# A three-block model on one core: turned values by transposing transfers instead of TensorE

## The chip, the cores and the metric

The kernel runs on one core of one Trainium2 chip. The metric is the device time of one execution in microseconds (us). The core's engines are TensorE (PE in the rows; PEld is its weight load), VectorE (DVE), ScalarE (ACT), GpSimd (POOL) and SyncE (SP), each with its own queue of instructions, and 16 DMA engines that all queues share.

## The reference

The kernel computes two networks in a row on a sequence of 256 tokens with 2048 channels, in fp32. The first has two layers (differential attention and an S5 state-space mixer), each followed by an MLP; the second is one hybrid layer (forgetting attention and an RWKV-7 scan). What bears on the change is:

```python
def sqrelu_mlp(h, w1, w2):
    a = jax.nn.relu(h @ w1)          # 2048 -> 8192
    return (a * a) @ w2              # 8192 -> 2048

for i in range(DEPTH):               # 2 layers; i = 0 attention, i = 1 S5 with a GLU
    h = rmsnorm(x, norm_mix[i])
    x = x + mix
    x = x + sqrelu_mlp(rmsnorm(x, norm_mlp[i]), mlp_w1[i], mlp_w2[i])
return rmsnorm(x, norm_final)        # then the second network, which begins with a norm
```

## The kernel before

**Weights.** Every product with a weight matrix runs in chunks of 512 output columns. A chunk is eight units of 256 rows of the weight, 512 KB each. SP loads a unit into one of four buffers `raw`; ScalarE casts it to its upper part `wH` (four buffers); VectorE subtracts to get the lower part `wL` (`split`). PE multiplies the activation's upper and lower parts (`xH`, `xL` or `hH`, `hL`) with them: 12 matmuls of 128x512 a unit, eight with `wH`, then four with `wL`, for two blocks of 128 tokens (`product`, L1025 to L1042). SP loads the next unit when its `raw` buffer has been split, ScalarE casts when PE has used the unit four before (`unit_used`). Chunks alternate between two pairs of PSUM banks `acc[0]` and `acc[1]`.

**Turning.** A product needs its activation with the channel on the partitions; norms and squares leave it with the token there. PE turns it with transposes into PSUM (`turn`, L1044 to L1049): a turn here is 512 channels of 256 tokens, eight transposes. ScalarE then copies the upper part out of PSUM (`high`), VectorE subtracts the lower part (`low`), which frees the PSUM bank (`group_free`).

**Norms.** A norm's operand is made a quarter (512 channels) at a time, while the product before it still runs: VectorE adds a chunk to `X`, multiplies by the gain into `xn` (`lead_gain`), PE turns the quarter in the middle of the next chunk (`lead_mid`), ScalarE and VectorE take it out (`lead_high`, `lead_low`). The factor 1/rms comes in later. The fourth quarter is turned after the second unit of the next product's first chunk; the first unit of that chunk waits until the first three quarters are there (`lead_first`).

**MLPs.** Each has four blocks of eight chunks: four with `w1`, whose results ScalarE passes through a relu and VectorE squares into `stg`, then four with `w2`. In the first MLP all four squares of a block are turned by PE, one in the middle of each next chunk. Between its chunks VectorE, ScalarE, PE and GpSimd also make the tables of the S5 mixer. In the second MLP PE turns only the fourth. For the other three GpSimd separates the 16-bit halves of the words (L948), writes them to DRAM as two planes, and SP reads them back with a transposing transfer (`turn_halves`, L564) into `hT`, which lies where `hL` lies; ScalarE copies `hH` from there and VectorE subtracts in place.

What sets the order is written out by hand: each engine's queue is in program order. Where a wait comes in it decides who waits.

## Time and profile before

| | |
|---|---|
| median of 3 runs | 2959.79 us (2957.3 to 2960.62) |
| the profiled execution | 2962.57 us, span 2960.9 us |
| busy: PE / PEld | 99% / 82% of the span |
| busy: VectorE / ScalarE / GpSimd | 60% / 47% / 14% |
| granted TensorE clock | 0.997 of full speed |
| mean DMA traffic | 199 GB/s |

The span is the time from the first to the last instruction of the profile; the execution's own time is 1.7 us longer. The MLPs take from 404 to 1129 us and from 1387 to 2092 us of it. A busy share is an average over the span; where one engine fills it, the others' shares count only where that engine waits for them.

### The profile page before, as it was taken

What the parts mean: (1) busy time and instruction counts of PE and PEld (TensorE: products, weight loads), DVE (VectorE), ACT (ScalarE), POOL (GpSimd) and SP (SyncE); (2) the same over time, 40 slices, a digit from 0 to 9 for tenths busy, and PEclk for the clock granted to TensorE, in tenths of its full rate; (3) what the DMA queues carried; (4) which work ended last, traced back from release to release, by engine and by line L of the source; (5) the groups of instructions that cost most, each with busy time, mean ns of one, the idle gap of its engine ahead of it and who ended that gap; (6) DMA issues with size and microseconds to landing.
All of it is one profiled execution on the core that took longest, in us unless ns stands there. A gap on an engine that the chain in (4) does not pass through costs nothing.

```text
span 2960.9 us, 44546 instructions
## 1 busy us (share of the span) xinstructions
PE 2916.6 (99%) x17539; PEld 2432.9 (82%) x17539; DVE 1777.8 (60%) x2032; ACT 1392.6 (47%) x1947; POOL 412.6 (14%) x460
## 2 busy tenths in 40 slices
PE   9999999999999999999999999999999999998898
PEld 7888788888888887888888888888888888887787
DVE  5555657765766666555555555556644666665765
ACT  5555544344443446444434434344544444653344
POOL 2000010891000675300101001010000001000000
PEclk9999999999999999999999999999999999999999
DMA  7555476775666887566867667686666667661364
GB/s 256 173 171 170 156 206 204 235 234 196 192 211 218 233 255 218 166 190 213 233 194 219 207 200 227 192 228 196 190 178 191 199 199 244 221 200 52 121 212 166
DMA packets 327915, 590.00 MB, mean 199 GB/s; under 512 B 46617, under 2 KB 65305, under 8 KB 326066
## 3 DMA queue, kind: packets, MB, share of 16 engines
q1 hardware_dynamic: 309792, 528.35, 58.4%
q0 software_dynamic: 12720, 49.37, 5.6%
q10 hardware_dynamic: 5218, 9.67, 0.9%
q8 instruction: 133, 2.18, 0.3%
q14 instruction: 52, 0.43, 0.0%
HBM read 546.96 MB, written 27.79 MB: 194 GB/s over the span
## 4 chain that ended last, share of the span: by engine, by line
PE 94%; DVE 2%; POOL 1%; DMA 1%; ACT 1%; issue 1%; SPq 0%; ACTq 0%; DVEq 0%; POOLq 0%
PE acc L1033 28%; PE acc L1040 28%; PE acc L1034 28%; PE tp L1048 2%; PE acc L1775 1%; PE acc L1768 1%; PE acc L1769 1%; DMA raw<-in_mlp_w_dram 1%; POOL zz L926 0%; POOL xs L932 0%; PE acc L1667 0%; PE wk L1677 0%; POOL zz L928 0%; PE tp L1677 0%; DMA gt<-g_scratch 0%
## 5 line engine op out<-in xcount | busy, mean ns | idle before, releaser
L2559 DVE TENSOR_TENSOR wL<-raw,wH 128x1024 fp32r<-128x1024 f32 (+1 forms) x968 | 1205.4, 1254 | 1071.9 <-ACT wH L1833 1069.5
L1833 ACT CAST wH<-raw 128x1024 fp32r<-128x1024 f32 (+1 forms) x968 | 1008.4, 1046 | 1341.9 <-PE acc L1040 1172.3
L1033 PE MATMUL acc<-wH,xH 128*128 128x512 f32 (+1 forms) x2208 | 863.4, 392 | 1.3 <-ACT wH L1833 1.3
L1034 PE MATMUL acc<-wH,xL 128*128 128x512 f32 (+1 forms) x2208 | 855.0, 388 | 0.0
L1040 PE MATMUL acc<-wL,xH 128*128 128x512 f32 (+1 forms) x2208 | 587.0, 388 | 0.0
L1033 PE MATMUL acc<-wH,hH 128*128 128x512 f32 x1472 | 575.5, 391 | 1.9 <-DVE hL L2620 1.9
L1034 PE MATMUL acc<-wH,hL 128*128 128x512 f32 x1472 | 572.9, 389 | 0.0
L1033 PEld LDWEIGHTS acc<-wH,xH 128*128 128x128 f32 x2208 | 414.9, 188 | 85.3 <-ACT wH L1833 1.3
L1034 PEld LDWEIGHTS acc<-wH,xL 128*128 128x128 f32 x2208 | 414.9, 188 | 83.0 <-issue 0.5
L1040 PEld LDWEIGHTS acc<-wL,xH 128*128 128x128 f32 x2208 | 412.5, 188 | 85.9 <-DVE wL L2559 0.5
L1040 PE MATMUL acc<-wL,hH 128*128 128x512 f32 x1472 | 393.5, 389 | 0.0
L1033 PEld LDWEIGHTS acc<-wH,hH 128*128 128x128 f32 x1472 | 276.4, 188 | 58.8 <-DVE hL L2620 2.4
L1040 PEld LDWEIGHTS acc<-wL,hH 128*128 128x128 f32 x1472 | 276.3, 188 | 57.4
L1034 PEld LDWEIGHTS acc<-wH,hL 128*128 128x128 f32 x1472 | 276.4, 188 | 56.4
L948 POOL COPY planes<-stgs 128x1024 uint16<-128x1024 uint16 x24 | 36.2, 1538 | 543.4 <-DVE stgs L2734 543.4
L960 POOL DMA_DIRECT2D prev<-stgs x8 | 4.3, 540 | 478.5 <-ACT stgs L2354 478.5
L787 POOL DMA_DIRECT2D sv<-in_b_a_re_dram x1 | 0.5, 545 | 383.7 <-PE tp L1048 383.7
L1768 PE MATMUL acc<-wH,xH 128*128 128x512 f32 x128 | 50.4, 394 | 1.2 <-DVE xL L2620 1.0
L1769 PE MATMUL acc<-wH,xL 128*128 128x512 f32 x128 | 49.8, 389 | 0.0
L2670 DVE SCALAR_TENSOR_TENSOR X<-acc,small,X 128x512 f32<-128x512 f32 x64 | 45.0, 744 | 0.5 <-PE acc L1040 0.4
L2734 DVE TENSOR_TENSOR stgs<-stgs,acc 128x512 f32<-128x512 f32 x64 | 40.9, 680 | 0.0
L2620 DVE TENSOR_TENSOR hL<-tp,hH 128x512 fp32r<-128x512 f32 x56 | 35.9, 682 | 7.6 <-ACT hH L1891 7.5
(547 smaller groups left out, 2242.2 us busy)
## 6 DMA issues: line engine op xcount, KB each, us to landing
raw<-in_mlp_w_dram SPq DMA_DIRECT2D x512, 512.0 KB, 4.2
raw<-in_w_in_dram SPq DMA_DIRECT2D x192, 512.0 KB, 4.3
raw<-in_a_w_in_dram SPq DMA_DIRECT2D x96, 512.0 KB, 3.9
raw<-in_b_w_glu_dram SPq DMA_DIRECT2D x64, 512.0 KB, 3.7
raw<-in_a_w_out_dram SPq DMA_DIRECT2D x32, 512.0 KB, 4.0
raw<-in_w_out_dram SPq DMA_DIRECT2D x32, 512.0 KB, 4.2
raw<-in_w_proj_fox_dram SPq DMA_DIRECT2D x16, 512.0 KB, 5.3
raw<-in_w_proj_rwkv_dram SPq DMA_DIRECT2D x16, 512.0 KB, 5.1
```

The lines of the kernel that those rows point to most:

```text
L948: nc.gpsimd.tensor_copy(dst[:, m], words).then_inc(halved, 1)
L1033: nc.tensor.matmul(bank, aH[:, k, rows], wH[:, j % SPLIT, u, 0:n], start=k == 0, stop=False)
L1034: nc.tensor.matmul(bank, aL[:, k, rows], wH[:, j % SPLIT, u, 0:n], start=False, stop=False)
L1040: last = nc.tensor.matmul(bank, aH[:, k, rows], wL[:, j % SPLIT, u, 0:n], start=False, stop=k == KT - 1)
L1048: last = nc.tensor.transpose(dst, src, ident[:])
L1768: nc.tensor.matmul(bank, xH[:, k, rows], wH[:, j % SPLIT, u], start=k % 8 == 0, stop=False)
L1769: nc.tensor.matmul(bank, xL[:, k, rows], wH[:, j % SPLIT, u], start=False, stop=False)
L1833: nc.scalar.copy(wH[:, j % SPLIT, :, 0:n], raw[:, j % RAW, :, 0:n]).then_inc(high_done, 1)
L2559: nc.vector.tensor_tensor(wL[:, j % SPLIT, :, 0:n], raw[:, j % RAW, :, 0:n], wH[:, j % SPLIT, :, 0:n].bitcast(F32), ALU.subtract).then_inc ...
L2620: nc.vector.tensor_tensor(dL, tp[bank][:], dH.bitcast(F32), ALU.subtract).then_inc(group_free, 1)
L2670: nc.vector.scalar_tensor_tensor(x, acc[par][m][:], rstd_sq[:, m:m + 1], x, ALU.mult, ALU.add).then_inc(acc_free, 1)
L2734: nc.vector.tensor_tensor(r, r, acc[c % 2][m][:], ALU.mult).then_inc(acc_free, 1)
```

## The change

Four kinds of values are no longer turned by PE: all squares of both MLPs, and the first three quarters of the operand of three norms (those before the first MLP, before the second MLP, and the last norm of the first network, which is also the second layer's). They go through DRAM as 16-bit planes and come back by transposing transfers. The halves of words are separated by VectorE in the first MLP (into the second half of `stg`, L2826 of the changed kernel), with ScalarE issuing the write; by GpSimd in the second MLP and for the norms. The transposing transfers, 16 per MLP and 9 for norms, stand in SP's queue between weight loads. The first two column blocks of the second product run as a pair: six units of the first, six of the second, then the last two of each, so that the fourth turned block is needed only from the thirteenth unit on. VectorE adds the first of the pair to `X` two units sooner than its partner. The fourth quarter of each norm, and all of the first norm, stay on PE.

```diff
-HALVED = 3
+LEADS = (1, 3, 4)
+MISSED = 2 * 8 * FB + 3 * 2 * (QT - 1)
+PAIRED = [(h, j) for h in range(2) for j in range(6)] + [(h, j) for h in range(2) for j in (6, 7)]
+SECOND = PAIRED + [(c, j) for c in (2, 3) for j in range(UNITS)]
...
+            def turn_lead(n, q, used):
+
+                sp.wait_ge(lead_out[q], 16 * n)
+                sp.wait_ge(unit_used, used)
+                sp.dma_start(xT[:, 4 * q:4 * q + 4].bitcast(U16), lead_dram[q].rearrange("t h n -> (t h) n"),
+                             transpose=True).then_inc(lead_in[q], 16)
+
...
+                enter = c0 * UNITS + SPLIT
 
                 def turn_halves(b, c):
 
-                    sp.wait_ge(plane_out[c], b * 16 + 16)
-                    sp.wait_ge(unit_used, b * 8 * UNITS + (c0 * UNITS + SPLIT))
+                    sp.wait_ge((plane_out if n0 else first_out)[c], 16 * (b + 1))
+                    sp.wait_ge(unit_used, enter + b * 8 * UNITS)
...
+                for b in range(FB):
                     for c in range(4):
                         for j in range(UNITS):
+                            if b == 0 and c == 0 and j == 5:
+                                lead(2)
+                            if c >= 2 and j == HALF:
                                 turn_halves(b, c - 2)
+                            load(b * 8 + c0 + c, j, w1v[j][:, :, b * D + c * NW:b * D + (c + 1) * NW])
+                    for v in range(4):
+                        for p in range(UNITS):
+                            if v < 2 and p == HALF:
+                                turn_halves(b, v + 2)
+                            if tail and b == FB - 1 and v == 3 and p in (3, 5):
+                                tail(p // 4)
+                            c, j = SECOND[v * UNITS + p]
+                            rows = w2[b * D + j * UK * P:b * D + (j + 1) * UK * P, c * NW:(c + 1) * NW]
+                            load(b * 8 + c0 + 4 + v, p, rows.rearrange("(k p) n -> p k n", p=P))
                 t.chunk += 8 * FB
+                t.mlps += 1
...
+            stream(I["a_w_out"][0], 4, lambda i, j: turn_lead(1, i - 2, used) if i >= 2 and j == 5 else None)
+            stream_mlp(I["mlp_w1"][0], I["mlp_w2"][0], lambda q: turn_lead(1, q, used))
...
+                    if c in (3, 5, 7) and j == 5:
+                        turn_lead(2, (c - 3) // 2, (c0 + 1) * UNITS + SPLIT)
...
+            def halves_of_lead(n):
+
+                for q in range(QT - 1):
+                    i = buffer_free()
+                    for m in range(MT):
+                        pool.wait_ge(xn_done, MT * (QT * LEADS[n - 1] + q) + m + 1)
+                        nc.gpsimd.tensor_copy(parted(planes[:, i])[:, m], halves_of(xn[:, m, q * NW:(q + 1) * NW])).then_inc(lead_halved, 1)
+                    pieces[1] += 1
+                    pool.wait_ge(lead_halved, MT * pieces[1])
+                    if n > 1:
+                        pool.wait_ge(lead_in[q], 16 * (n - 1))
+                    reading[i] = (lead_out[q], 16 * n)
...
+                def paired(b, after):
+
+                    c, fill = b * 8 + (c0 + 4), b * 8 + (f0 + 4)
+                    for p, (h, j) in enumerate(PAIRED):
+                        if p in (0, 6):
+                            pe.wait_ge(acc_free, fill * 2 + 2 * h + 2)
+                        if p == UNITS and after:
+                            after(4)
+                        if h == 0:
+                            pe.wait_ge(group_free, b * 8 + (g0 + j + 3))
...
+                        product(b * 8 + (c0 + c), b * 8 + (f0 + c), c % 2, xH, xL, first=first if c == 0 else None)
...
             def lead_high(q):
+                if q < QT - 1 and t.norm > 1:
+                    act.wait_ge(lead_in[q], 16 * (LEADS.index(t.norm - 1) + 1))
                 for g in (2 * q, 2 * q + 1):
-                    high(t.lead + g, None, g % 2, xH[:, 2 * g:2 * g + 2])
+                    if q < QT - 1 and t.norm > 1:
+                        nc.scalar.copy(xH[:, 2 * g:2 * g + 2], xT[:, 2 * g:2 * g + 2]).then_inc(group_high, 1)
+                    else:
+                        high(t.lead + g, None, g % 2, xH[:, 2 * g:2 * g + 2])
...
+                    def halves(c):
+                        n = 4 * b + c
+                        act.wait_ge(halved_first, MT * (n + 1))
+                        act.dma_start(by_token(plane_dram[c]), halved_rows).then_inc(first_out[c], 16)
+
                     for c in range(8):
-                        if c or not entry:
+                        if after and 1 <= c <= 4:
+                            split(b * 8 + (c0 + c), 1, units=(4,))
+                            halves(c - 1)
+                            split(b * 8 + (c0 + c), 1, units=(5, 6, 7))
+                        elif c or not entry:
                             split(b * 8 + (c0 + c), 1)
...
                         split(b * 8 + (c0 + c + 1), 0, units=(0, 1, 2) if last else None)
-                        if halves and c == 3:
-                            turned_halves(2)
+                        if 1 <= c <= 4:
+                            turned(c - 1)
+                        if tail and c >= 6:
...
                 lead_square(c - 1)
+                split(c0 + c + 1, 0)
                 lead_high(c - 1)
-                split(c0 + c + 1, 0)
...
+                        if c == 5:
+                            dve.wait_ge(unit_used, b * 8 * UNITS + ((c0 + 4) * UNITS + 14 + SPLIT))
+                            add_to(b * 8 + (f0 + 4), 0, 0, tail)
...
+                            if after:
+                                n = 4 * b + c
+                                if n:
+                                    dve.wait_ge(first_out[(n - 1) % 4], 16 * ((n - 1) // 4 + 1))
+                                for m in range(MT):
+                                    dve.wait_ge(acc_free, b * 16 + (2 * (f0 + c) + 5 + m))
+                                    nc.vector.tensor_copy(halved_rows[:, m], halves_of(stg[:, 0, m])).then_inc(halved_first, 1)
...
                 split(c0 + c, 1)
+                split(c0 + c + 1, 0)
                 lead_low(c - 1)
-                split(c0 + c + 1, 0)
```

ScalarE at the entry of the first MLP, in the order of its queue; `wH<-raw` is the cast of a unit, `xH<-tp` the copy of a turned quarter out of PSUM, `wk,small<-X` the square of a quarter for its norm. Before:

```order
L1937 ACTIVATE wk,small<-X 128x512 [waits sumsq_done,acc_free]
L1937 ACTIVATE wk,small<-X 128x512
L1891 CAST xH<-tp 128x512 [waits group_done] x2
L1833 CAST wH<-raw 128x1024 [waits unit_used,raw_in0]
L1833 CAST wH<-raw 128x1024 [waits unit_used,raw_in1]
L1833 CAST wH<-raw 128x1024 [waits unit_used,raw_in2]
L1833 CAST wH<-raw 128x1024 [waits unit_used,raw_in3]
L1833 CAST wH<-raw 128x1024 [waits unit_used,raw_in0]
L1833 CAST wH<-raw 128x1024 [waits unit_used,raw_in1]
```

After, from the same square on:

```order
L2016 ACTIVATE wk,small<-X 128x512 [waits sumsq_done,acc_free]
L2016 ACTIVATE wk,small<-X 128x512
L1906 CAST wH<-raw 128x1024 [waits unit_used,raw_in0]
L1906 CAST wH<-raw 128x1024 [waits unit_used,raw_in1]
L1906 CAST wH<-raw 128x1024 [waits unit_used,raw_in2]
L1906 CAST wH<-raw 128x1024 [waits unit_used,raw_in3]
L2003 CAST xH<-xT 128x512 [waits lead_in2]
L2003 CAST xH<-xT 128x512
L1906 CAST wH<-raw 128x1024 [waits unit_used,raw_in0]
```

The copy of the third quarter stood ahead of the casts of the next chunk's first four units; now it comes from `xT` and stands behind them.

VectorE at the end of the first MLP's second chunk: `wL<-raw,wH` is the split of a unit, `hL<-...` the lower part of turned squares, `stgs<-stgs,acc` the squares, `sv` a step of the S5 tables. Before:

```order
L2559 TENSOR_TENSOR wL<-raw,wH 128x1024 [waits high_done] x3
L2620 TENSOR_TENSOR hL<-tp,hH 128x512 [waits group_high] x2
L2559 TENSOR_TENSOR wL<-raw,wH 128x1024 [waits high_done] x4
L2734 TENSOR_TENSOR stgs<-stgs,acc 128x512 [waits relu_done] x2
L2917 TENSOR_TENSOR sv<-sv 128x64 [waits s5_act]
```

After:

```order
L2644 TENSOR_TENSOR wL<-raw,wH 128x1024 [waits high_done] x7
L2799 TENSOR_TENSOR hL<-hT,hH 128x512 [waits group_high] x2
L2819 TENSOR_TENSOR stgs<-stgs,acc 128x512 [waits relu_done] x2
L2826 COPY stgs<-stgs 128x1024 [waits acc_free,first_out0]
L2826 COPY stgs<-stgs 128x1024 [waits acc_free]
L3008 TENSOR_TENSOR sv<-sv 128x64 [waits s5_act]
```

The subtraction of the turned squares moved from the middle of the chunk to its end, and two copies that separate the halves came in ahead of the S5 steps.

PE in the middle of the first MLP's second chunk, before; `tp<-ident,stgs` is a transpose of squares:

```order
L1040 MATMUL acc<-wL,xH 128x512 [waits split_done]
L1040 MATMUL acc<-wL,xH 128x512 x3
L1048 MATMUL tp<-ident,stgs 128x128 [waits group_free,acc_free]
L1048 MATMUL tp<-ident,stgs 128x128 x3
L1048 MATMUL tp<-ident,stgs 128x128 [waits group_free]
L1048 MATMUL tp<-ident,stgs 128x128 x3
L1033 MATMUL acc<-wH,xH 128x512 [waits high_done]
```

After:

```order
L1098 MATMUL acc<-wL,xH 128x512 [waits split_done]
L1098 MATMUL acc<-wL,xH 128x512 x3
L1091 MATMUL acc<-wH,xH 128x512 [waits high_done]
L1092 MATMUL acc<-wH,xL 128x512
```

The eight transposes are gone; nothing took their place.

## Rows read from the trace of the kernel before

**Rows 1.** The page: the chain that ended last, share of the span by engine.

```profile
PE 94%; DVE 2%; POOL 1%; DMA 1%; ACT 1%; issue 1%; SPq 0%; ACTq 0%; DVEq 0%; POOLq 0%
```

**Rows 2.** PE's timeline around one turn: start us, busy us, line, what.

```profile
457.90 1.07 PE L1040 MATMUL acc<-wL,xH 128*128 128x512 f32 x4
460.62 1.07 PE L1040 MATMUL acc<-wL,xH 128*128 128x512 f32 x4
...
464.24 1.07 PE L1040 MATMUL acc<-wL,xH 128*128 128x512 f32 x4
```

**Rows 3.** Instructions on `hT`: count, ns min/median/max, first and last start.

```profile
L1964 ACT CAST hH<-hT x24: 615/616/619, 1445.0 to 2003.0; 128x512 fp32r<-128x512 f32 x24
L2709 DVE TENSOR_TENSOR hL<-hT,hH x24: 682/685/689, 1446.2 to 2004.4; 128x512 fp32r<-128x512 f32 x24
L564 SPq DMA_TRANSPOSE hT<-plane_scratch x12: 3239/3592/5628, 1425.0 to 1993.5; - x12
...
DMA to landing us min/median/max: 5.2/5.6/7.8
```

**Rows 4.** The timeline of all engines where the second MLP ends.

```profile
2091.92 0.39 PE L1033 MATMUL acc<-wH,xH 128*128 128x512 f32 x1
...
2092.17 1.05 ACT L1833 CAST wH<-raw 128x1024 fp32r<-128x1024 f32 x1 [1.67 <-PE acc L1040]
...
2093.25 1.22 DVE L2559 TENSOR_TENSOR wL<-raw,wH 128x1024 fp32r<-128x1024 f32 x1 [1.50 <-ACT wH L1833]
...
2094.39 0.74 DVE L2670 SCALAR_TENSOR_TENSOR X<-acc,small,X 128x512 f32<-128x512 f32 x1
```

**Rows 5.** Groups of instructions: count | busy us, mean ns | idle before.

```profile
L3001 DVE COPY FW<-cT 128x1024 f32<-128x1024 f32 x2 | 1.4, 694 | 0.1
...
L948 POOL COPY planes<-stgs 128x1024 uint16<-128x1024 uint16 x24 | 36.2, 1538 | 543.4 <-DVE stgs L2734 543.4
```

**Rows 6.** The page: one group of DMA issues, last its median us to landing.

```profile
plane_scratch<-planes POOLq DMA_DIRECT2D x12, 512.0 KB, 5.2
```

**Rows 7.** VectorE's timeline behind chunks 1 and 19 of the first MLP.

```profile
455.11 0.23 DVE L2917 TENSOR_TENSOR sv<-sv 128x64 f32<-128x64 f32 x1 [0.42 <-ACT sv L2160]
...
462.30 4.63 DVE L2559 TENSOR_TENSOR wL<-raw,wH 128x1024 fp32r<-128x1024 f32 x4
...
864.71 0.29 DVE L3013 TENSOR_TENSOR sk<-eye,skT 128x128 f32<-128x128 f32 x1
...
871.04 1.23 DVE L2559 TENSOR_TENSOR wL<-raw,wH 128x1024 fp32r<-128x1024 f32 x1
```

**Rows 8.** The timeline behind chunk 0 of the first MLP.

```profile
440.17 2.36 DVE L2559 TENSOR_TENSOR wL<-raw,wH 128x1024 fp32r<-128x1024 f32 x2
...
441.45 0.50 PE L1040 MATMUL acc<-wL,xH 128*128 128x512 f32 x1
```

**Rows 9.** Stretches: busy PE, PEld, DVE, ACT, POOL, clock, DMA share, GB/s.

```profile
613.00:635.00 22.00, 22.00 (x102) 18.29 (x101) 10.61 (x11) 7.94 (x9) 20.25 (x26) 1.00 0.94 264
1053.00:1075.00 22.00, 22.00 (x99) 18.21 (x98) 13.68 (x11) 8.45 (x11) 20.43 (x18) 1.00 1.00 293
1413.00:1435.00 22.00, 22.00 (x99) 18.22 (x98) 11.30 (x11) 9.61 (x11) 3.77 (x3) 1.00 0.84 241
1501.00:1523.00 22.00, 22.00 (x99) 18.22 (x98) 11.36 (x11) 8.39 (x8) 0.00 (x0) 1.00 0.62 195
```

**Rows 10.** ScalarE's timeline: casts that waited for a load (idle us in brackets).

```profile
631.87 1.05 ACT L1833 CAST wH<-raw 128x1024 fp32r<-128x1024 f32 x1 [3.72 <-DMA raw<-in_mlp_w_dram]
636.45 1.05 ACT L1833 CAST wH<-raw 128x1024 fp32r<-128x1024 f32 x1 [3.52 <-DMA raw<-in_mlp_w_dram]
...
1072.27 1.05 ACT L1833 CAST wH<-raw 128x1024 fp32r<-128x1024 f32 x1 [4.68 <-DMA raw<-in_mlp_w_dram]
```

**Rows 11.** The timeline where the S5 tables end: GpSimd, then VectorE.

```profile
1083.14 0.58 POOL L901 DMA_DIRECT2D r_scratch<-tmade  x1 [0.30 <-POOL tmade L900]
...
1089.12 1.28 DVE L2644 TENSOR_TENSOR xn<-X,gains 128x512 f32<-128x512 f32 x2
```

More of the change, by code:

```diff
@@ L1042, in product, with turn @@
                     last.then_inc(unit_used, 1)
-            def turn(n, blocks, count=1):
+            def turn(n, blocks):
                 pe.wait_ge(group_free, n + 1)
@@ L1113, in block_of @@
+                def block_of(b, first=None, after=None):
                     for c in range(4):
[L1114 to L1115 removed]
+                        product(b * 8 + (c0 + c), b * 8 + (f0 + c), c % 2, xH, xL, first=first if c == 0 else None)
                         if after:
                             after(c)
[L1118 to L1121 removed]
+                    paired(b, after)
+                    for c in range(2, 4):
+                        product(b * 8 + (c0 + 4 + c), b * 8 + (f0 + 4 + c), c % 2, hH, hL)
@@ L1255, in _ @@
             for c in range(13, 16):
-                product(c0 + c, f0 + c, c % 2, hH, hL, mid=lead_mid(c - 13))
+                product(c0 + c, f0 + c, c % 2, hH, hL)
             def s5_turns(c):
@@ L1419, in _ @@
             for c in range(1, 8):
-                product(t.chunk + c, t.fill + c, c % 2, hH, hL, mid=lead_mid(c // 2 - 1) if c in (2, 4, 6) else None)
+                product(t.chunk + c, t.fill + c, c % 2, hH, hL)
             t.chunk += 8
```

249 lines of the change are left out of this document (128 added, 121 removed).

## The prediction

> **What bounds the kernel now.** I read first the chain that ended last [rows 1]: the reader is to see 94% of it on TensorE (PE), which is busy 99% of the span. So time is won only by taking instructions from PE's own queue, and lost wherever PE is made to wait. Second, PE's timeline over one turn of eight transposes [rows 2]: without one the last matmuls of two units begin 2.72 us apart (460.62 - 457.90), with one 3.62 us (464.24 - 460.62). A turn is worth 0.90 us of PE, and nothing hides it. Third, the waits around the weights: at which time after PE's units the other engines do their work, which tells how late each may be.
>
> **What goes.** The first MLP loses 16 turns (four blocks of four), the second 4 (its fourth column block), three norms 3 each: 29 turns, 232 transposes, 29 x 0.90 = 26.1 us. Every matmul stays; the paired order of two column blocks of the second product changes which bank a unit goes to and costs nothing by itself. In the second MLP the rest of the path exists for three pieces of four: a transposing transfer takes SP 3.2 to 5.6 us to issue and lands 5.6 us after, ScalarE's copy takes 0.62 and VectorE's subtraction 0.69 [rows 3], and PE is busy 22.00 of 22 us beside it [rows 9]. So I count the 4 turns there as pure gain: the fourth piece is needed twelve units after its chunk ends, and GpSimd, which gets 3.8 us more per block, has 3.8 of 22 us of work in a stretch with a piece.
>
> **What is added.** (a) *Entry of a product behind a norm.* PE's first unit there waits for `group_free` of all three early quarters (`lead_first`, j of 0), and that wait stays. Until now the third quarter was done in the middle of the chunk before. Now ScalarE copies it after its casts of the new chunk's first four units, and the fourth cast can only begin when PE has finished the old chunk, since it needs that unit's `wH` buffer. Rows 4 show the end of such a chunk: PE's new chunk begins at 2091.92, the fourth cast at 2092.17, VectorE's split of it at 2093.25, the next VectorE instruction at 2094.39. ScalarE's two copies (0.62 each) end at about 2094.3; VectorE's two subtractions (0.69 each, about 0.6 apart) run from 2094.39 to 2095.7. So PE starts 3.8 us late. That is so at the entry of the first MLP and of the second layer's first product: 7.6 us. At the second MLP's entry the third quarter is copied one chunk earlier, and nothing waits. The data is in time by a small margin: from the chunk's start, 2.5 to the last split's end, about 1.3 each for two subtractions, two additions and two products with the gain (6.4); GpSimd's copies 3.1 and the write's issue and landing 5.9 [rows 5, 6] make 15.4; SP has its place for the transfer at 16, and it lands at 21.6; ScalarE asks for it at 21.8 + 1.3 = 23.1.
>
> (b) *VectorE late in the first MLP.* After a chunk's end T it now does, before the next chunk's fifth unit: the last split (to T+2.5, as in rows 4), two subtractions moved here from mid-chunk (1.2), two squares (1.2), two separating copies, its S5 work W, then the split (1.14 to the next start). PE wants that split at T + 4 x 2.72 + 1.8 = T+12.7. The copy (1024 words of 16 bits, every second one read) has no row on VectorE. Bounds: below, a copy of 1024 fp32 words, 0.69; above, GpSimd's copy of just this pattern, mean 1.54 [rows 5]; between them the split (1.22, two tensors read [rows 4]). I take 0.69, the row of the same engine, operation and count: two are 1.25 back to back. W is read between the starts [rows 7]: 455.11 to 462.30 in chunk 1 is 7.2; 864.71 to 871.04 in chunk 19 is 6.3. Chunk 1: 2.5 + 1.2 + 1.2 + 1.25 + 7.2 + 1.14 = 14.5, so PE waits 1.8. Chunk 19: 13.6, so 0.9. All others end before 12.7, chunk 3 last with 0.4 to spare; there each tenth that the copies take longer comes through. Chunk 0 has no cover: its loads were late, VectorE's split began at 440.17 and PE's matmul on it at 441.45 instead of 441.24 [rows 8]. Without the turn PE wants it at 440.35; with the copies it is there at 440.17 + 1.25 + 1.14 = 442.6: 2.2, of which 0.2 was paid before. Together 1.8 + 0.9 + 2.0 = 4.7 us.
>
> The Trainium skill, *VectorE: DVE Perf Modes*, section "What auto-detection actually checks", says that 16-bit packing needs a step of 1, but that a one-source instruction in SBUF whose outermost dimensions are even may use both read ports, two elements a cycle. By that page's table this copy is an estimate of 0.70 us, which agrees with the 0.694 in rows 5; if only the first half held, the estimate would be about 1.2 and (b) some 3.5 us more.
>
> (c) *Late weight loads.* Each turned piece adds a write and a transposing read of 0.5 MB. In the second MLP a stretch with both shows a DMA share of 0.84, one without 0.62 [rows 9]: 0.22 x 22 = 4.8 us of all engines per piece. ScalarE casts a unit as soon as its buffer is free, 6.9 us before PE must have the cast begun (three units less 0.25 and 1.05): that is the cushion. Two stretches of the first MLP that get pieces are full already, 0.94 and 1.00. In the first, two casts in a row waited 3.72 and 3.52 instead of the usual 1.67 [rows 10], 3.9 late in all; the excess of 0.16 x 22 = 3.5 makes 7.4, 0.5 over. In the second a cast was 3.0 late; with 4.8 it is 7.8, 0.9 over. For the flood of S5 table loads at the first MLP's entry I allow 0.6 more. Sum 2.0; its ends are 0 and 34 (last rival).
>
> (d) *Costed at nothing.* ScalarE's 16 plane writes: each waits some 2.5 us for VectorE, against four units of cover. In chunk 29 VectorE waits for S5 tables of which GpSimd issues the last at 1083.14; with a landing as in rows 6 they were there 0.8 us before VectorE's work at 1089.12 [rows 11]. PE gets there four turns (3.6) sooner and the tables start 1.25 later, so VectorE waits 4.1 and ends its next split at about T+11.5, inside 12.7. Without that cover it is 1 to 3 us.
>
> **Sum.** 26.1 - 7.6 - 4.7 - 2.0 = 11.8 us. The profiled execution took 2962.57 (span 2960.9 and 1.7 around it, which stays); it becomes 2950.8. It was 2.8 over the median of 2959.79, so a median is forecast at 2948.0.
>
> **Rivals.** *The entry wait doesn't show.* For it: 7.6 us rest on an order of instructions, not on a row. Against: rows 4 show the fourth cast behind PE's last unit. Then 2948.0 - 7.6 = 2940.4. *The copy is slow.* For it: its source is read with a stride, and GpSimd takes 1.54. Two copies of 1.22 are 1.05 more per chunk: 3.2 in chunks 0, 1 and 19, 0.7 in chunk 3, 0.1 to 0.4 in two more; at 1.54 about double: 2952 to 2956. *The loads starve PE*, the rival on the slow side. Its place is the first MLP's queue of raw loads; it decides when a cast is more than 6.9 us late, and from there each piece costs PE its full 4.8. Seven of the sixteen pieces fall in stretches with a share of 0.8 or more (the first and the last whole stretch are in rows 9). 7 x 4.8 = 33.6: 2982. Against: outside the table flood no cast before came over 3.9 late, and the second MLP runs at 0.84 without a wait. The Trainium skill, *DMA: Bandwidth & Descriptors*, section "Issuing engines are not separate DMA queues", speaks for this rival: ScalarE's issuing frees issue time alone, since all queues share the same 16 engines. The shares of rows 9, higher by what a piece moves, agree.
>
> **How the numbers follow.** Forecast case 0.55, own range 2943 to 2954; no entry wait 0.08; slow copy 0.20; starving loads 0.12; anything else 0.05. A measurement of this kernel tells about 0.2% (5.9 us) from no change: faster means under 2953.9, slower over 2965.7. Faster: 0.53 + 0.08 + 0.07 of the slow copy = 0.68. Same: 0.13 of the slow copy, 0.02 of the forecast, 0.04 of the rest = 0.19. Slower: 0.12 + 0.01 = 0.13. The range 2939 to 2960 takes in the first three cases and leaves out the starving loads.
>
> **What would show it.** On PE 232 fewer transposes; blocks of the second MLP 64 x 2.72 = 174.1 apart; idle of 3.8 us released by VectorE's `xL` at the entries of the first MLP and of the second layer, none at the second MLP's; waits for `wL` of 1 to 2 us at the fifth unit of chunks 1, 2 and 20 of the first MLP. On VectorE 32 copies of 0.69. I am wrong if the copies take over 1.1, if casts in the first MLP wait over 7 us for `raw`, or if the two entries cost under 2 us or over 5.

## The result: slower, and the profile after

The changed kernel takes 2977.16 us (median of 8 runs, 2967.28 to 2995.12) where the kernel before takes 2959.38 (8 runs, 2956.02 to 2964.30): a ratio of 1.0065, 95% interval 1.0046 to 1.0083. Run again with the experiments it took 2969.87 (7 runs, 2966.38 to 2986.57), ratio 1.0046 (1.0028 to 1.0065). It is slower by 10 to 18 us, and its times scatter over 28 us where those of the kernel before scatter over 8. I had forecast 2948.0, and 2939 to 2960 as the range.

The profiled execution took 2992.68 us, one of the long ones. Its page:

```profile
span 2991.0 us, 43255 instructions
...
PE 2905.8 (97%) x17307; PEld 2417.5 (81%) x17307; DVE 1829.2 (61%) x2064; ACT 1393.3 (47%) x1947; POOL 459.7 (15%) x499
...
PE 88%; DVE 5%; DMA 4%; ACT 1%; issue 1%; SPq 1%; POOL 0%; ACTq 0%; DVEq 0%; POOLq 0%
```

The turns did go: PE has 17307 matmuls, 232 fewer. Its busy time fell from 2916.6 to 2905.8, by 10.8 and not by 26.1, so 15.3 us of its matmuls ran slower. Its idle time (span less busy) grew from 44.3 to 85.2 us, by 40.9. 15.3 + 40.9 - 26.1 = 30.1 us, the difference of the spans. And where 94% of the chain of waits lay on PE [rows 1], it is 88% now; VectorE and the transfers have the rest.

The stretches tell where. Ahead the first MLP and ahead of that the attention, behind it the mixer and the second MLP (busy us of PE, PEld, DVE, ACT, POOL, PE's clock, DMA share, GB/s); first the kernel before, then the changed one:

```profile
404.00:1129.00 725.00, 724.08 (x3533) 601.16 (x3532) 477.63 (x502) 310.59 (x348) 258.53 (x250) 1.00 0.72 221
1387.00:2092.00 705.00, 704.13 (x3140) 583.49 (x3139) 387.87 (x375) 311.53 (x347) 45.86 (x38) 1.00 0.71 212
```

```profile
404.00:1129.00 725.00, 687.91 (x3256) 566.73 (x3257) 489.38 (x520) 294.82 (x328) 245.07 (x234) 0.97 0.80 233
1387.00:2092.00 705.00, 703.40 (x3107) 582.04 (x3106) 398.07 (x368) 310.83 (x343) 69.16 (x56) 1.00 0.75 222
```

In the first MLP PE was idle for 0.9 us and is now for 37.1, at a mean clock of 0.97. In the second it is idle for 1.6 us. (Both kernels are read over the same times, while the changed kernel's MLPs end some 33 and 22 us later; in what the stretches leave out PE has no wait over 0.4 us.) The second MLP is as forecast: from relu to relu of the same chunk one block later its rows lie 174.03 us apart (174.1 forecast, 174.92 before).

```profile
1439.08 1.08 ACT L2073 ACTIVATE stgs<-acc 128x512 f32<-128x512 f32 x2
...
1613.11 1.08 ACT L2073 ACTIVATE stgs<-acc 128x512 f32<-128x512 f32 x2
```

PE's long waits in the changed kernel, from its timeline (start us, busy us, in brackets the idle time before and what ended it):

```profile
406.65 0.47 PE L1091 MATMUL acc<-wH,xH 128*128 128x512 f32 x1 [3.70 <-issue]
...
445.73 1.19 PE L1098 MATMUL acc<-wL,xH 128*128 128x512 f32 x4 [1.29 <-DVE wL L2644]
...
469.47 1.20 PE L1098 MATMUL acc<-wL,xH 128*128 128x512 f32 x4 [1.68 <-DVE wL L2644]
...
665.98 0.79 PE L1091 MATMUL acc<-wH,xH 128*128 128x512 f32 x1 [19.95 <-ACT wH L1906]
...
896.03 2.08 PE L1182 MATMUL acc<-wL,hH 128*128 128x512 f32 x4 [2.15 <-DVE wL L2644]
...
1056.66 2.07 PE L1098 MATMUL acc<-wL,xH 128*128 128x512 f32 x4 [4.32 <-DVE wL L2644]
...
1081.47 1.19 PE L1182 MATMUL acc<-wL,hH 128*128 128x512 f32 x4 [1.38 <-DVE wL L2644]
...
1105.13 0.77 PE L1175 MATMUL acc<-wH,hH 128*128 128x512 f32 x1 [3.40 <-ACT wH L1906]
...
2117.92 0.76 PE L1091 MATMUL acc<-wH,xH 128*128 128x512 f32 x1 [4.30 <-DVE xL L2736]
```

These nine are 42.2 us. The first and the last are my term (a), the ones for `wL` at 445, 469 and 896 my term (b). The 19.95 at 646 (it ends at 665.98), and the group from 1056 on, lie at or behind the two full stretches for which term (c) allowed 1.4 us in all.

A wait costs more than itself. Behind the last row PE's next unit begins at 2122.28, so this one took 4.36 us and not 2.72; behind the first, 4.36 as well (406.65 to 411.01). In both, most of these matmuls begin 0.43 us apart instead of 0.23, and the granted clock is 0.50 in the stretches 408 to 411 and 2118 to 2121: the lower of its two levels, 1.2 of 2.4 GHz. So each of these two waits has 1.64 us of slow clock behind it.

**The event at 646 us.** So I call what happens before the longest wait. GpSimd issues its four reads of the S5 input matrix, SP a microsecond later the transposing transfer of block 1's first piece. GpSimd, then SP, then ScalarE:

```profile
626.26 4.64 POOL L857 DMA_DIRECT2D bT<-bb_scratch  x4
```

```profile
627.17 15.91 SPq L595 DMA_TRANSPOSE hT<-plane_scratch  x1
643.13 28.90 SPq L561 DMA_DIRECT2D raw<-in_mlp_w_dram  x8
```

```profile
661.02 1.14 ACT L2041 CAST hH<-hT 128x512 fp32r<-128x512 f32 x2 [23.55 <-DMA hT<-plane_scratch]
```

SP needs 15.91 us to issue that transfer, where before the change 3.2 to 5.6 were seen [rows 3]. For so long no weight load is issued. The transfer lands 33.8 us after its issue (5.6 before); ScalarE, whose next casts stand behind that copy, waits 23.55 us for it. And all 16 DMA engines are busy and move little:

```profile
630.00:640.00 10.00, 10.00 (x46) 8.28 (x45) 3.68 (x3) 2.96 (x3) 9.01 (x15) 1.00 1.14 144
640.00:650.00 10.00, 6.03 (x27) 4.67 (x25) 0.00 (x0) 0.00 (x0) 8.67 (x18) 1.00 1.26 68
650.00:660.00 10.00, 0.00 (x0) 0.00 (x0) 0.00 (x0) 0.00 (x0) 8.41 (x21) 0.50 1.02 181
```

144 and 68 GB/s at shares (the next to last figure) of 1.14 and 1.26. In the kernel before the same four reads landed in 12.0 us (median) beside 274 GB/s; here it is 27.7.

### The profile page after: what moved, and what is told of

It reads as the page before. It is cut to its first block, busy times and chain, and to the rows that moved or that the text cites. A ratio compares the mean times of both kernels' runs of the same rounds, so it can differ in the third digit from the quotient of the medians.

```text
span 2991.0 us, 43255 instructions
## 1 busy us (share of the span) xinstructions
PE 2905.8 (97%) x17307; PEld 2417.5 (81%) x17307; DVE 1829.2 (61%) x2064; ACT 1393.3 (47%) x1947; POOL 459.7 (15%) x499
## 4 chain that ended last, share of the span: by engine, by line
PE 88%; DVE 5%; DMA 4%; ACT 1%; issue 1%; SPq 1%; POOL 0%; ACTq 0%; DVEq 0%; POOLq 0%
PE acc L1091 22%; PE acc L1098 22%; PE acc L1092 22%; PE acc L1182 4%; PE acc L1175 3%; PE acc L1176 3%; DMA hT<-plane_scratch 1%; DMA raw<-in_mlp_w_dram 1%; DVE wL L2644 1%; PE acc L1848 1%; PE acc L1841 1%; PE acc L1842 1%; PE tp L1106 1%; SPq L595 1%; PE wk L1417 1%
## 5 line engine op out<-in xcount | busy, mean ns | idle before, releaser
L2644 DVE TENSOR_TENSOR wL<-raw,wH 128x1024 fp32r<-128x1024 f32 (+1 forms) x968 | 1228.8, 1282 | 998.6 <-ACT wH L1906 995.5
L988 POOL COPY planes<-stgs 128x1024 uint16<-128x1024 uint16 x32 | 48.3, 1539 | 547.8 <-DVE stgs L2819 547.8
L1001 POOL COPY planes<-xn 128x1024 uint16<-128x1024 uint16 x18 | 30.4, 1716 | 532.2 <-DVE xn L2729 532.2
```

Source lines behind the costliest of these rows:

```text
L988: nc.gpsimd.tensor_copy(parted(planes[:, i])[:, m], halves_of(stg[:, 0, m])).then_inc(halved, 1)
L1001: nc.gpsimd.tensor_copy(parted(planes[:, i])[:, m], halves_of(xn[:, m, q * NW:(q + 1) * NW])).then_inc(lead_halved, 1)
L2644: nc.vector.tensor_tensor(wL[:, j % SPLIT, :, 0:n], raw[:, j % RAW, :, 0:n], wH[:, j % SPLIT, :, 0:n].bitcast(F32), ALU.subtract).then_inc ...
```

## The experiments

All times are medians of the runs of one batch, with the kernel before on the same chip in each batch (2958.0 to 2960.0 us). Versions of different batches are compared too; up to 2.0 us of such a difference may be the batch's. A "piece" is one turned column block of squares; (1,0) is block 1's first. "By unit" is the edit of the fourth one; it is in all from the sixth on.

**The changed kernel again.**

> The changed kernel again, as the partner of the three kernels below on the same chip. Its trace has one wait of PE of 19.95 us at 646 us, and its eight times run from 2967 to 2995. If that wait is one collision of transfers that hits some executions harder than others, the times scatter by 10 us or more again (2965 to 2995) while those of the kernel before stay within 5. If the loss is a steady lack of transfer bandwidth, the times stay within 5 us too.

Measured: 2969.87 us, 2966.38 to 2986.57. The scatter is there again (below I call a time long that is over 8 us above its version's median). In its trace the wait at 646 is 1.30 us: the event has many sizes. SP's transfer stands 1.8 us ahead of the reads there, where it stood 0.9 behind. A wait of 9.88 us at 1081 is new.

**Reads in long rows.**

```diff
-pool.dma_start(bT[:, r, :, twice], bb_dram.rearrange("(k e) c r s -> r (e c) k s", e=8)[r])
+half = slice(twice * (KT // 2), (twice + 1) * (KT // 2))
+pool.dma_start(bT[:, r, half].rearrange("p k a s -> p (k a s)"), <the same bytes, 4 KB per partition>)
```

> GpSimd's four reads bT<-bb_scratch take the same bytes, 4 x 512 KB, from and into long contiguous rows in place of rows of 256 bytes (S5's input matrices come out wrong). Theory one, the third quarter-piece's transposing transfer and these reads choke each other because of their many small packets: the wait of 19.95 us at 646 and the slow clock behind it (2 us) go, the reads land within 15 us instead of 27.7, the median falls by 8 to 20 us to about 2960 to 2968, and the times scatter by under 8 us. Theory two, the bytes of the turned pieces are too many for the DMA engines in the first MLP: the bytes are the same, so the wait stays at 15 to 20 us and the median at 2977.

Measured: 2967.14 us, 2960.95 to 2972.92. SP is held for 10.57 us by the transfer, yet the wait at 646 is 0.97; no time is long, but the median fell by 2.7 alone, where theory one had 8 to 20. So the event seems to make the long times, and something steady the rest. Whether the rows or chance kept the event away can't be told from this run.

**One transposing transfer later.**

```diff
+if t.mlps == 0 and b in SHIFTED:                    # SHIFTED = (1,)
+    if c == 3 and j in (0, HALF):
+        turn_halves(b, j // HALF)
-if c >= 2 and j == HALF:
+elif c >= 2 and j == HALF:
...
-if 1 <= c <= 4: turned(c - 1)
+for i in ((), (), (0,), (1, 2), (3,), (), (), ())[c]: turned(i)      # block 1, ScalarE and VectorE
```

> In the first MLP's second block alone, SP issues the first piece's transposing transfer four units later (behind GpSimd's bT reads instead of among them), and ScalarE and VectorE take the pieces 0 and 1 one chunk later each; all bytes and all packets stay. Theory one (a collision in time): PE's wait at 646 falls from 19.95 us to under 3, the median by 8 to 20 us. Theory two (too many bytes in this stretch): the wait only moves, PE still loses 10 us or more between 640 and 700, the median stays within 4 us of the changed kernel's.

Measured: 2969.59 us, 2962.82 to 2981.17. In its trace the wait at 646 is gone, as theory one had it, although SP is held for 12.79 us by the transfer; the median did not move, as theory two had it, but nothing of the 10 us or more that theory two wanted between 640 and 700 is there. One of the nine times is long (2981.17), with the transfer 9.1 us behind the reads. So the event is not what makes the median of this batch.

**Wait by unit at the entries.**

```diff
 def lead_first(j):
-    if j == 0:
-        pe.wait_ge(group_free, t.lead + 8)
     if j == 2:
         lead_turn(3)
-    if j >= 6:
-        pe.wait_ge(group_free, t.lead + j + 3)
+    pe.wait_ge(group_free, t.lead + j + 3)
```

> PE's first chunk behind an early-turned norm waits before each unit for that unit's own group alone, not for all three early quarters before the first. My term (a): the waits of 3.70 us at the first MLP's entry and 4.30 at the second layer's go, and with them 1.64 us each in which the clock is at half: 11.3 us less than the changed kernel, about 2966. Rival (the third quarter is the late thing, not the form of the wait): PE starts at once but waits about as long at the fifth unit, and the time falls by under 3 us.

Measured: 2957.72 us (12 runs, 2953.11 to 2971.44), 12.2 less than its partner; of the two waits 0.62 and 0.74 us are left in the trace. Term (a) is right in place and cause.

**The first MLP by PE again.**

```diff
+def own_turn(b, c):
+    pe.wait_ge(acc_free, 2 * (f0 + 8 * b + c) + 6)
+    turn_stg(g0 + 8 * b + 2 * c, 0)
...
+mid=(lambda: own_turn(b, c - 1)) if after and c and b not in TURNED else None     # TURNED = ()
```

(With it VectorE's copies, ScalarE's writes and SP's transposing transfers of the blocks that are not in `TURNED` go, and their upper parts are copied from PSUM as before.)

> The first MLP's sixteen pieces go by PE's transposes again (no copy on VectorE, no write by ScalarE, no transposing transfer there); the second MLP and the three norms as in the changed kernel, with its wait at the entries. Theory one, nearly all that the change loses over its entry waits is lost in the first MLP: PE gets 14.4 us of turns back there and loses the waits of the trace partner, 1.29, 1.68, 1.30, 0.46, 1.91, 3.95, 1.28 and 9.88, some 22 with 3 of slow clock: 8 us less than its partner, about 2962 beside 2969.9. Rival: the waits are there because norms and second MLP shifted the program; then they stay, and the time rises by 14 to about 2984.

Measured: 2961.43 us (11 runs, 2959.07 to 2966.63), no time long. As expected, to 0.6 us; in the first MLP, behind the entry, its trace has no wait of PE over 0.4.

**Both.**

> The edit of the run before together with the wait by unit at the entries, 11.3 us less by the trace: if the two losses are independent, 2962 - 11.3 = 2951; no long wait of PE is left outside the last layer. If the entry's cost had hidden something (late weights at the start of the first MLP), under 8 us less than the run before.

Measured: 2952.80 us (2949.47 to 2955.34), ratio to the kernel before 0.9977 (0.9968 to 0.9986). The entry gave 8.6 here, not 11.3; its trace has 0.74 us at the second layer's entry in its place and 1.68 of "issue" at 1733.

**Blocks 0 and 2, then 0 to 2, by transfers** (`TURNED = (0, 2)` and `(0, 1, 2)`).

> Wait by unit at the entries, and in the first MLP the blocks 0 and 2 by transposing transfers, 1 and 3 by PE's transposes. Theory one, each block stands by itself: blocks 0 and 2 save 7.2 us of turns and cost the waits 1.28 + 1.69 and 1.80 (4.8): 2.4 less than the run before, about 2949, with no wait over 2 us. Rival (the load on the DMA engines accumulates over the MLP): the waits of block 0 and 2 shrink or move, the time is within 1 us of the run before or above it.

> As the run before, and block 1 by transfers too: 3.6 us of turns less against waits of 1.2 + 0.9 us in a quiet execution and up to 20 where the transposing transfer meets the reads bT<-bb_scratch. If the collision is what scatters the times: median within 2 us of the run before, some times 5 to 20 us above the median, which the run before has not. If block 3 alone scatters them: as close together as in the run before.

Measured: 2955.75 (2951.89 to 2958.22) and 2952.94 us (2945.42 to 2976.66). The first is a miss by 7 us: two blocks by transfers cost 3 more than none. Its waits for `wL` are 1.26, 1.69 and 2.96, and at the second layer's entry it waits 2.46. The second has the long times again (2961.34, 2976.66), which the first has not; 2 of 12 beside 0 of 11 can be chance, but it points to block 1. Against the version with block 3 as well (2957.72) it gains 4.8 us although PE does 3.6 us more of turns: block 3 by transfers costs 8.4, by two batches.

**Eight quiet pieces.** (`TURNED` as pairs of block and piece: (0,2), (0,3), (1,1), (1,2), (1,3), (2,0), (2,1), (2,2).)

> Wait by unit at the entries; in the first MLP eight pieces go by transposing transfers (pieces 2 and 3 of block 0, 1 to 3 of block 1, 0 to 2 of block 2), chosen where the traces show neither S5 work on VectorE behind the chunk, nor the bT reads, nor GpSimd's tensor work; the other eight go by PE's transposes. Theory (a piece costs only where one of these three meets it): 8 x 0.90 = 7.2 us less than all sixteen by PE (2952.8), about 2946, no wait over 1 us in the first MLP. Rival (each transposing transfer costs PE about what its turn saves, by the load on the DMA engines): within 2 us of 2952.8.

Measured: 2950.17 us (2944.68 to 2951.56): 2.6 less than all by PE, between the two theories. PE's waits in the first MLP are 0.54 for `wL` and 1.44 of "issue"; at the second layer's entry PE waited 3.26, 2.5 more than there.

**Short copies.**

```diff
+x = slice(0, 8 if n else NW)
-nc.vector.tensor_copy(halved_rows[:, m], halves_of(stg[:, 0, m]))
+nc.vector.tensor_copy(halved_rows[:, m, :, x], halves_of(stg[:, 0, m])[:, :, x])
```

> All sixteen pieces by transfers, wait by unit at the entries; VectorE's separating copies, but for the first piece's, copy 8 columns of each half instead of 512 (the hidden values come out wrong), transfers unchanged. Theory (late VectorE): of the partner's waits (2957.7 us) the 1.69, 1.80, 3.95 and 0.96 for wL go, and the 5.85 for a cast in block 3, which starts from copies that are late beside GpSimd's work, falls under 2: 10 to 15 us less, 2943 to 2948. Rival (block 3's transfers are slow by themselves, by the table writes and reads of GpSimd): the wait of 5.85 stays at 4 or more and the time falls by 5 to 9, to 2949 to 2953.

Measured: 2951.22 us (2946.59 to 2962.24), 6.5 less than in the batch before. Its profiled execution is the longest one. There the waits of 1.80 and 3.95 for `wL` are gone. The one behind chunk 1 stays (1.58 for 1.69), against the theory: with short copies VectorE stands 0.66 us for ScalarE's S5 step `sv`, which the full ones had covered. And ScalarE's casts are late as before:

```profile
646.49 0.80 PE L1091 MATMUL acc<-wH,xH 128*128 128x512 f32 x1 [7.47 <-ACT wH L1903]
...
1050.73 0.47 PE L1172 MATMUL acc<-wH,hH 128*128 128x512 f32 x1 [2.56 <-ACT wH L1903]
...
1083.31 0.77 PE L1172 MATMUL acc<-wH,hH 128*128 128x512 f32 x1 [10.11 <-ACT wH L1903]
```

So the rival holds for block 3: the late transfers there are not the late copies' doing.

**Reads in shorter rows, with and without transfers.**

```diff
+for part in (slice(0, S5_P // 2), slice(S5_P // 2, S5_P)):
+    pool.dma_start(bT[:, r, :, twice, part], bb_dram.rearrange("(k e) c r s -> r (e c) k s", e=8)[r, :, :, part])
```

> Blocks 0 to 2 by transfers, wait by unit; the four reads bT<-bb_scratch are cut into eight with rows of 128 bytes instead of 256: the same bytes in twice as many packets. Theory (the transposing transfer and reads in short rows choke each other): the wait at 644 grows from 2.40 us to 10 or more in the profile and the median rises by 8 to 20 us over 2952.9. Rival (only the bytes count, or the late times come from elsewhere): within 3 us of 2952.9.

> The same short rows of 128 bytes, with all sixteen pieces by PE's transposes: no transposing transfer is near the reads. Theory: the reads land later, but PE does not wait, and the time is within 3 us of 2952.8, so that what the kernel before this one shows beyond that belongs to the meeting of both. Rival (the short rows alone starve the weights): 8 us or more above 2952.8.

Measured: 2953.37 (2948.78 to 2973.59) and 2954.42 us (2948.59 to 2960.21). The theory is down for the median: twice the packets move that of the first by 0.4. Its trace says nothing of the meeting, since SP's transfer came 1.8 us ahead of the reads. Three of its eleven times are long (2967.19, 2969.43, 2973.59), none of the second's.

**VectorE's order at the second layer's entry.**

```diff
-    for q in (0, 1) if c == 6 else (2,):
-        lead_low(q)
+if tail and c == 6:
+    lead_low(0)
+    lead_low(1)
...
 add_to(b * 8 + (f0 + c), c % 2, c - 4, tail)
+if tail and c == 7:
+    lead_low(2)
```

> The eight quiet pieces by transfers and the wait by unit; and at the end of the second MLP VectorE adds and multiplies the last quarter before it subtracts the third one, whose transposing transfer is late. In the partner's trace (2950.2 us) PE's turn of the last quarter waited 3.26 us there, behind that subtraction. If the order is what costs: 2 to 3 us less, about 2947.5. If the late transfer alone counts (PE needs the third quarter before that turn anyway): within 1 us of 2950.2.

Measured: 2945.23 us (5 runs, 2944.52 to 2945.89), 4.9 less, of which 2.0 may be the batch (the kernel before took 2960.0 in that one and 2958.0 in this); the wait is 0.84. Ratio to the kernel before 0.9952 (0.9939 to 0.9966). This is the best version, by five runs.

**Which piece, and with which reads.** (Pieces of blocks 0 to 2 without (1,0); blocks 0 to 2 with the long rows; (1,0) alone.)

> Blocks 0 to 2 by transfers but for block 1's first piece, which goes by PE's transposes. Theory (the high times come from that piece's transposing transfer, which is issued 1 us behind the reads bT<-bb_scratch): none of some eleven times is 8 us over the median, median within 2 us of 2952.9. Rival (any piece of block 1, or the load of all): one to four of eleven are high, as with all twelve (2 of 12, 3 of 11).

> Blocks 0 to 2 by transfers, all pieces; the four reads bT<-bb_scratch in long contiguous rows (S5's input matrices come out wrong). Theory (rows of 256 bytes or less are half of the collision): none of the times is 8 us over the median. Rival (only that the transfers meet, whatever their rows): two or three of eleven are high.

> Of the first MLP's sixteen pieces block 1's first alone goes by transfers, with the wait by unit at the entries. Theory (this one meeting makes the high times): median 2952 to 2954, and one to four of eleven times 8 to 25 us above it, where all sixteen by PE had none. Rival (it needs the load of the other pieces): no high times.

Measured: 2949.55 (6 runs, 2947.51 to 2952.65), 2953.73 (2948.91 to 2958.18) and 2952.97 us (2950.58 to 2956.33). No long time in any. That is what the theories had for the first two; with six runs the first is a weak test, and its median lies 3.4 under 2952.9, where 2 were allowed. The third goes against its theory: the piece alone makes no long times in eleven runs, though SP is held for 15.45 us by it in the trace. Whether the other pieces' load is what lacks there, no run shows.

**The transfer ahead of the reads, and behind them.**

```diff
-if c >= 2 and j == HALF:
+if c >= 2 and j == (5 if (b, c) == (1, 2) and not t.mlps else HALF):     # and 3 in place of 5
```

> The best version so far (2945.2 us, eight quiet pieces) with block 1's first piece by transfers as well, its transposing transfer one unit earlier in SP's order (2.7 us), so that it is issued ahead of the reads bT<-bb_scratch. Theory (what makes the event is reads first, transposing transfer behind them): no high times, SP issues it in under 6 us, and the median is 0 to 1 us under 2945.2. Rival (order does not matter): one or more of some ten times is 8 us high, or the issue takes 10 us or more.

> Blocks 0 to 2 by transfers as in the run of 2952.9 us, whose transposing transfer at 620.47 us stood 1.8 us ahead of the reads and was issued in 4.80 us; here it is one unit later in SP's order, so behind the reads in nearly every execution. Theory: SP is held 12 to 16 us by it, PE waits at about 644 us for 5 to 20 us, the median rises by 8 to 20 us to 2961 or more, and the high case is now the usual one. Rival (order does not matter): median within 3 us of 2952.9 and as few high times as there.

Measured: ahead 2949.47 us (12 runs, 2940.62 to 2962.27), behind 2968.47 (10 runs, 2958.50 to 2981.92). One unit later costs 15.5 us of the median against the run with blocks 0 to 2, and nine of the ten times are over 8 us above that run's median. Ahead is a miss: one time is long, and the median is 4.2 over the 2945.2 that it was to keep; only SP's 5.18 us came as expected. The two traces, first the run with blocks 0 to 2 (transfer at 620.47, reads from 622.27), then the one behind (reads from 620.37, transfer at 624.00). The first view ends at 624.0 and so has two of the four reads:

```profile
620.47 4.80 SPq L599 DMA_TRANSPOSE hT<-plane_scratch  x1
...
622.27 2.35 POOL L861 DMA_DIRECT2D bT<-bb_scratch  x2
...
644.47 0.50 PE L1096 MATMUL acc<-wH,xH 128*128 128x512 f32 x1 [2.40 <-ACT wH L1915]
```

```profile
620.37 4.63 POOL L861 DMA_DIRECT2D bT<-bb_scratch  x4
...
624.00 14.92 SPq L599 DMA_TRANSPOSE hT<-plane_scratch  x1
...
643.39 1.14 ACT L2058 CAST hH<-hT 128x512 fp32r<-128x512 f32 x2 [12.98 <-DMA hT<-plane_scratch]
...
646.50 0.79 PE L1096 MATMUL acc<-wH,xH 128*128 128x512 f32 x1 [6.35 <-ACT wH L1915]
```

Over the twelve traces with this piece by a transfer the two kinds don't mix. Where SP's transfer was issued ahead of the reads it held SP for 4.25 to 5.18 us (six traces), where it was issued behind them for 10.57 to 16.28 (six: 0.9, 1.7, 3.6, 4.5, 4.5 and 9.1 us behind).

SP's hold is not what stops PE, though. In block 2 another transfer of GpSimd's, its 2 MB write of S5 powers, is issued 4.1 to 4.6 us ahead of the transposing transfer of piece (2,1), and that one holds SP for 11.51 to 12.65 us in all fifteen traces that have this piece by a transfer, the best version's among them. In the changed kernel:

```profile
846.45 2.74 POOL L911 DMA_DIRECT2D f_scratch<-FW  x1 [173.09 <-DVE FW L3099]
...
850.61 12.08 SPq L595 DMA_TRANSPOSE hT<-plane_scratch  x1
```

PE doesn't wait for it; the transfer lands 15.6 us after its issue. For piece (1,0) PE's longest wait goes with the landing: 33.8 us after issue with a wait of 19.95, 23.2 with 7.47 (short copies), 19.4 with 6.35 (the transfer behind), 17.4 with 2.27 (the piece alone), 13.9 with 0.97 (long rows), 9.4 to 11.3 where the transfer went first, with 0 to 2.40.
The version with the transfer put first is not better than the one without it (2945.23): PE waited 1.30 + 1.28 + 1.12 us there, and its times still scatter, which no trace of mine explains.

## Why the prediction was wrong

**What goes: right in the stretch that can be read.** 232 transposes, and 174.03 us per block of the second MLP. The fourth piece there costs nothing. In the whole time it came less full: with the first MLP by PE and the wait by unit 13 turns are gone, 11.7 us, which makes 2947.4 of the 2959.1 before, and 2952.8 was measured. Of these 5.4 us its trace has 3.6 in four waits (0.62, 0.74, 0.53, 1.68); the rest is not accounted for.

**(a) The entries: right, and mis-sized.** The waits are 3.70 and 4.30 us where I had 3.8 each, at the places I named, with none at the second MLP's. I left out the slow clock behind them, 1.64 each: 11.3 us, not 7.6. Removing them gave 12.2 in one batch and 8.6 in another. The margin that I called small in the third quarter's data is small: with the wait gone, PE's turn of the last quarter waited 0.74 to 5.00 us behind VectorE's subtraction of the third, and with that subtraction behind the last quarter it waited 0.84.

**(b) VectorE: the copy right, the places half, the sum too small.** The copies' row is what I took (0.69; two in a row are 1.29 for 1.25):

```profile
L2826 DVE COPY stgs<-stgs x32: 681/686/1668, 441.2 to 1077.6; 128x1024 uint16<-128x1024 uint16 x32
```

Chunk 0 cost 1.29 us (2.0 forecast), chunk 1 1.68 (1.8), chunk 19 2.15 (0.9). Chunk 1's figure is right, but not by the copies: without them it still was 1.58, since VectorE then stands 0.66 us for ScalarE's S5 step (0.42 before the change [rows 7]), a wait that the sum had nowhere. The 1.25 more of chunk 19 are a weight load 0.9 us late and a turned piece 0.3 late, so of the kind of (c). But the longest copy is 1668 ns, and of block 3's chunks I had said that they "end before 12.7". There GpSimd is busy for 99.84 of 129 us on S5 tables, and VectorE's instructions last longer beside it: seven splits in a row 15.56 us, 2.2 each for 1.23 elsewhere, and two copies 3.14.

```profile
1051.26 3.14 DVE L2826 COPY stgs<-stgs 128x1024 uint16<-128x1024 uint16 x2
1054.32 15.56 DVE L2644 TENSOR_TENSOR wL<-raw,wH 128x1024 fp32r<-128x1024 f32 x7
```

```profile
1000.00:1129.00 129.00, 119.91 (x508) 97.94 (x508) 101.47 (x76) 51.80 (x60) 99.84 (x76) 0.96 0.93 263
```

The Trainium skill, *SBUF — State Buffer*, section "Who interferes with whom", says that VectorE and GpSimd share a pair of SBUF ports under an exclusive lock; these rows agree, in that the same instructions of VectorE last 1.8 times (splits) to 2.4 times (the longest copy, 1668 ns for 686) as long there. The kernel before has splits of 2.0 to 2.3 us in the same stretch, which I had in view and didn't add up: eight splits at 2.2 with two squares, two copies (3.1) and two subtractions (3.1) are 25 us, past a chunk's 21.8. That fits the 4.32 at 1056, and with short copies the wait is gone. All the copies together are worth 6.5 us (the short ones), against 4.7 for the whole of (b).

**(c) Late loads and transfers: this step failed.** I took 2.0 us, with 34 as the other end, priced by the bytes that a piece adds to the DMA engines; with (b)'s 4.7 that made 6.7 for the first MLP, where the medians give 19 (below). Two assumptions were in it. The first is that a transposing transfer takes SP 3.2 to 5.6 us and lands after 5.6, as in the second MLP. In the first it took 4.5 to 15.9 and landed after 6.5 to 33.8:

```profile
L595 SPq DMA_TRANSPOSE hT<-plane_scratch x16: 4507/5700/15913, 449.6 to 1088.2; - x16
...
DMA to landing us min/median/max: 6.5/8.0/33.8
```

The second MLP was the wrong row to go by: GpSimd issues little there but the pieces' writes. In the first it reads and writes S5's tables. Where one of these, 2 MB in all, was issued first, SP is held two to four times as long and the weight loads queue behind it; where the piece then lands late as well, ScalarE's copy holds the casts. That the order matters the run with the transfer behind shows (15.5 us); that it isn't all, the one with it ahead, whose times scatter over 22 us. In the seven versions whose first piece of block 1 goes by PE none of 62 times is long, with it by a transfer 15 of 124. The second assumption is that lateness shows in the cast for which a load is late, and (d) counted for ScalarE's queue only the piece writes. It came through that queue: casts stood behind a copy whose transfer had not landed. Block 3, where the DMA share was 0.90 before anything was added, has a wait of PE for a cast in all six traces that have it by transfers; the execution of the repeat run waited 9.88 us there:

```profile
1067.98 9.07 SPq L595 DMA_TRANSPOSE hT<-plane_scratch  x1
```

```profile
1087.70 1.14 ACT L2041 CAST hH<-hT 128x512 fp32r<-128x512 f32 x2 [11.84 <-DMA hT<-plane_scratch]
```

By the runs without and with block 3 it is 8.4 us in the median, copies included. SP's hold is not needed for it: with short copies the piece took SP 5.42 us, landed after 16.2, and PE waited 10.11.

**The rival of starving loads** had the side, the place (the raw loads of the first MLP) and, with 2982, nearly the time, and I gave it 0.12. Its mechanism, 4.8 us for each of seven pieces by their bytes, is not what happened: with long rows, the same bytes, the event was absent, and for three pieces of block 1 by transfers PE waited nowhere. So the time that it gives is near by luck. What I wrote against it, that the second MLP runs at a share of 0.84 without a wait, was the same wrong row.

**The account of the median,** from the medians of the partner runs. All by PE in the first MLP and by unit: 2952.8. The entries' wait: 8.6 to 12.2. The first MLP by transfers: 4.9 (2957.7) where the event is rare, with 14.4 us of turns saved inside it; so about 19 us of waits and slow clock, for 6.7 forecast. 2957.7 + 12.2 = 2969.9. Against the forecast of 2948.0 that is 12.6 us more in the first MLP, 4.6 more at the entries, and the 5.4 of "what goes": 22.6, where 21.9 were measured. In the first batch four of eight times were over 2980, and the median was 2977: 7.3 more, which I put down to the event, seen there in one trace.

**Left open:** what in the meeting of reads and transfer makes it (with long rows none of 21 times was long, with rows of 256 or 128 bytes 7 of 30 in the versions that are otherwise the same; and with the transfer behind the reads the engines moved 298 GB/s from 630 to 640 us with long rows, 127 to 221 in four traces with short ones: that points to the rows and doesn't settle it); why the piece alone makes no long times; which of block 3's table transfers makes its pieces late; and the 5.4 us above. No version without the table transfers was tried.

## The version that beats both

Wait by unit, eight quiet pieces, VectorE's last quarter first: 2945.2 us. Its first MLP:

```profile
404.00:1129.00 725.00, 720.26 (x3503) 597.44 (x3502) 487.34 (x530) 314.72 (x363) 266.27 (x254) 1.00 0.78 235
```

4.7 us idle of 725, for 37.1 in the changed kernel. The kernel before has 0.9 there, with 16 turns where this one has 8.

## What to carry to other kernels

A transfer's issue and landing times hold for the stretch where they were read; before taking them elsewhere, look at which other queues have transfers in flight there, and in which order they start. A long issue is a sign of it; how late the data lands is what the readers feel. When a value comes by a transfer and not from the engine before, the copy that takes it is a wait in an in-order queue: put it as late as its reader allows, and count what stands behind it. And when PE is made to wait at all, add the slow clock behind the wait.

## What was not expected of the hardware

- A transposing transfer of 0.5 MB issued behind GpSimd's four 0.5 MB reads holds SP for 10.57 to 16.28 us; ahead of them for 4.25 to 5.18. Behind a 2 MB write of GpSimd's it holds SP for 11.51 to 12.65 in every trace.
- While both are in flight the 16 DMA engines show shares of 1.14 to 1.26 and move 144 to 68 GB/s in the changed kernel's trace, 127 to 221 at 1.11 to 1.19 (630 to 640 us) in three others with the transfer behind; without the transfer, 274 GB/s at 1.01.
- The same kernel's executions then differ by 28 us (2967.28 to 2995.12), with the clock of the whole run between 0.991 and 0.997; by PE's transposes in the first MLP they differ by 6 to 12.
- A wait of PE of 3.7 to 20 us is followed by a unit of 4.36 to 4.97 us in place of 2.72.
